# Wider column tiles and a folding matmul for the modulation rows of a two-layer diffusion trunk

## The reference, cut to what matters

```
sh1, sc1, g1, sh2, sc2, g2         = adaln(c,         ada_w[i], ada_b[i])   # silu(c) @ ada_w + ada_b, split in six
csh1, csc1, cg1, csh2, csc2, cg2   = adaln(c_ctx_row, ada_w[i], ada_b[i])
hl = modulate(rms_norm(xl, norm1_g[i]), sh1, sc1)
xl = xl + g1 * mixer(...);  xl = xl + g2 * conv_ffn(modulate(rms_norm(xl, norm2_g[i]), sh2, sc2), ...)
```

## Time and profile before

| | |
|---|---|
| median of 3 runs | 1913.11 us |
| profiled execution, time | 1913.11 us |
| profiled execution, span from first to last instruction | 1911.3 us |
| mean granted TensorE clock | 0.984 of 2.4 GHz |
| TensorE busy | 95% of the span |
| VectorE, ScalarE, GpSimd busy | 60%, 35%, 4% |
| modulation products L485 | 1536 records (768 matmuls) |
| modulation turns L478 | 24 records |

### The profile page before, as it was taken

The page is one execution under the profiler, slowest core; times in us unless marked ns, Lnnn a source line. Parts: engine busy times, 40 slices in busy tenths (PEclk is TensorE's granted clock), DMA queues, the critical chain, the costliest instruction groups (busy, mean ns, idle before and its releaser), DMA issues.

```text
span 1911.3 us, 29443 instructions
## 1 busy us (share of the span) xinstructions
PE 1815.1 (95%) x12484; PEld 1563.5 (82%) x12484; DVE 1150.3 (60%) x1917; ACT 676.9 (35%) x1007; POOL 79.5 (4%) x146
## 2 busy tenths in 40 slices
PE   3999999999977999999999999999888999999997
PEld 3999999999966878888888888878655888888885
DVE  3465576657684486633655256567555498487485
ACT  3333334433422243312332123334677243233242
POOL 0000000000040000000000000000353000000000
PEclk8999999999998999999999999999999999999998
DMA  7221221122101123233333233212100223222322
GB/s 295 85 82 67 89 84 62 67 89 89 57 34 34 56 79 124 96 102 119 111 112 109 89 122 110 78 60 87 34 1 1 88 78 99 99 91 98 99 92 107
DMA packets 45346, 166.03 MB, mean 87 GB/s; under 512 B 4897, under 2 KB 5281, under 8 KB 45089
## 3 DMA queue, kind: packets, MB, share of 16 engines
q1 hardware_dynamic: 45216, 164.16, 24.9%
HBM read 162.05 MB, written 2.10 MB: 86 GB/s over the span
## 4 chain that ended last, share of the span: by engine, by line
PE 87%; DVE 7%; ACT 2%; issue 1%; DMA 1%; SPq 0%; POOL 0%; DVEq 0%; ACTq 0%
PE slot L428 31%; PE slot L417 9%; PE slot L419 8%; PE slot L418 8%; PE slot L845 4%; PE slot L847 4%; PE slot L846 4%; PE MA L585 3%; PE MB L485 2%; PE MA L847 2%; PE MA L846 2%; PE MA L845 2%; PE slot L798 1%; DMA AD<-in_ada 1%; DVE Y L1346 1%
## 5 line engine op out<-in xcount | busy, mean ns | idle before, releaser
L1260 DVE TENSOR_TENSOR WL<-WR,WH 128x1024 fp32r<-128x1024 f32 x204 | 249.4, 1224 | 223.6 <-ACT WH L900 222.4
L900 ACT ACTIVATE WH<-WR 128x1024 fp32r<-128x1024 f32 x204 | 215.4, 1056 | 381.3 <-DMA WR<-in_w 381.1
L417 PE MATMUL slot<-HH,WH 128*128 128x384 f32 (+2 forms) x848 | 302.6, 357 | 18.9 <-DVE HL L1353 11.3
L418 PE MATMUL slot<-HL,WH 128*128 128x384 f32 (+2 forms) x848 | 293.3, 346 | 0.0
L419 PE MATMUL slot<-HH,WL 128*128 128x384 f32 (+2 forms) x848 | 293.2, 346 | 0.0
L428 PE MATMUL slot<-HH,WH 128*128 128x256 f32 (+1 forms) x816 | 212.6, 342 | 2.5 <-DVE ACC L1580 1.6
L428 PE MATMUL slot<-HH,WL 128*128 128x256 f32 (+1 forms) x816 | 210.8, 340 | 0.0
L428 PE MATMUL slot<-HL,WH 128*128 128x256 f32 (+1 forms) x816 | 208.9, 338 | 0.0
L417 PEld LDWEIGHTS slot<-HH,WH 128*128 128x128 f32 x848 | 161.0, 190 | 38.8 <-issue 17.8
L428 PEld LDWEIGHTS slot<-HH,WH 128*128 128x128 f32 x816 | 151.8, 189 | 26.1 <-issue 7.1
L428 PEld LDWEIGHTS slot<-HL,WH 128*128 128x128 f32 x816 | 154.0, 189 | 18.1
(11 more groups left out here) (222 smaller groups left out, 2985.2 us busy)
## 6 DMA issues: line engine op xcount, KB each, us to landing
WR<-in_w SPq DMA_DIRECT2D x204, 512.0 KB, 3.4
ada_raw<-in_ada SPq DMA_DIRECT2D x84, 512.0 KB, 4.6
AD<-in_ada SPq DMA_DIRECT2D x3, 2048.0 KB, 23.5
X<-in_x SPq DMA_DIRECT2D x1, 3072.0 KB, 12.3
out<-Y SPq DMA_DIRECT2D x8, 256.0 KB, 2.2
Y<-in_masks SPq DMA_DIRECT2D x1, 512.0 KB, 19.7
rope<-in_rope SPq DMA_DIRECT2D x1, 512.0 KB, 4.1
small<-in_small SPq DMA_DIRECT2D x1, 327.5 KB, 3.0
```

What stands on the lines that cost most here:

```text
L417: mm(SLOT[s][:, po], WH[w % NB][:, k, :], hi[:, k, to], start=(k == 0), stop=False)
L418: mm(SLOT[s][:, po], WH[w % NB][:, k, :], lo[:, k, to], start=False, stop=False)
L900: go(WH[t % NB][:, :, :], WR[t % NB][:, :, :], ACT.Copy).then_inc(w_hi_done, 1)
L1260: tt(WL[t % NB][:, :, :], WR[t % NB][:, :, :], WH[t % NB][:, :, :].bitcast(F32), ALU.subtract).then_inc(w_split, 1)
```

## The change

Three things are laid out differently; the values computed are the same.

1. In `ada_products` the column tile is no longer chosen by the piece of the output but by the block of input channels: each matmul multiplies one block of 128 channels with all 512 output columns and accumulates in partitions 32f to 32f+31 (f is the number of the block modulo 4). A group is 8 matmuls of 512 columns instead of 32 of 128 columns. The four partial sums lie one below the other in PSUM.
2. The copy by ScalarE takes 128x512 instead of 128x128.
3. The turn becomes four float32 matmuls. Piece m of the row block (128x128) is the stationary operand, and the moving operand is `fold`, a 128x2 matrix with ones where the partition modulo 32 equals the column. This adds the four partial sums and transposes at once; eight useful values per partition land in `MB[:, 512:520]`. VectorE makes `fold` from the identity with three small additions before the first squares, and TensorE waits for it once.

```
-                turn(MB[:, 512:512 + P], ada_row(rows.now(1))[:, 0:P], ident[:, :]).then_inc(ada_turned, 1)
+                for m in range(4):
+                    last = mm(MB[:, 512 + 2 * m:514 + 2 * m], ada_row(rows.now(1))[:, m * P:(m + 1) * P], fold[:, :], start=True, stop=True)
+                last.then_inc(ada_turned, 1)
 ...
                 for f in range(4):
                     c = 2 * k + f
-                    for m in range(4):
-                        last = mm(MB[32 * m:32 * m + 32, 0:P], silu_w[:, c, :], src(f)[:, m * P:(m + 1) * P], start=(c == 0), stop=(c == KC - 1))
+                    last = mm(MB[32 * f:32 * f + 32, 0:512], silu_w[:, c, :], src(f), start=(k == 0), stop=(k == 2))
 ...
-                    pe.wait_ge(ident_in_done, 16)
+                    pe.wait_ge(fold_ready, 1)
 ...
-                go(ada_row(rows.now(1))[:, 0:P], MB[:, 0:P], ACT.Copy).then_inc(ada_copied, 1)
+                go(ada_row(rows.now(1))[:, 0:512], MB[:, 0:512], ACT.Copy).then_inc(ada_copied, 1)
 ...
-                go(ada_row(g)[:, 0:P], MB[:, 0:P], ACT.Copy).then_inc(ada_copied, 1)
+                go(ada_row(g)[:, :], MB[:, 0:512], ACT.Copy).then_inc(ada_copied, 1)
 ...
-                tt(ada[:, j:j + 4, :], MB[:, 512:512 + P].rearrange("p (m x) -> p m x", x=32)[:, :, 0:2],
+                tt(ada[:, j:j + 4, :], MB[:, 512:520].rearrange("p (m v) -> p m v", v=2),
 ...
+            link(tt(fold[:, :], ident[:, 0:2], ident[:, 32:34], ALU.add))
+            link(tt(fold[:, :], fold[:, :], ident[:, 64:66], ALU.add))
+            tt(fold[:, :], fold[:, :], ident[:, 96:98], ALU.add).then_inc(fold_ready, 1)
```

More of the change, by code:

```diff
@@ L132, in trunk @@
         silu_w = sb("silu_w", [P, KC, 32])
+        fold = sb("fold", [P, 2])
         ada = sb("ada", [P, 96, 2])
@@ L156, in trunk @@
             AD0 = sb("AD0", [P, 4 * ADA_FIRST - 4, 2, 512], F32, s)
-            row0 = sb("row0", [P, P], F32, s)
+            row0 = sb("row0", [P, 512], F32, s)
         with ExitStack() as s:
@@ L176, in trunk @@
             ACC = [sb(f"ACC{i}", [P, TOK], F32, s) for i in range(2)]
-            row2 = sb("row2", [P, P], F32, s)
+            row2 = sb("row2", [P, 512], F32, s)
         with ExitStack() as s:
@@ L221, in trunk @@
         sig_ready, silu_ready, lb_shifted = sem("sig_ready"), sem("silu_ready"), sem("lb_shifted")
+        fold_ready = sem("fold_ready")
         ada_copied, ada_turned, ada_ready = sem("ada_copied"), sem("ada_turned"), sem("ada_ready")
```

## The result

The changed kernel takes 1933.9 us (median of 5 runs, 1929.02 to 1937.39), the kernel before, run beside it, 1912.98 us (median of 5). The ratio is 1.0102, 95% interval 1.0084 to 1.0121: 1% slower, some 19.5 us. The forecast was 1928 us.

The account below looks back on a forecast made before the run. TensorE was taken to bound the kernel. Products -0.6, turns +14.2 and prologue +1.0 us summed to +14.6 us on 1913.1 us, giving 1927.7 us, stated as 1928 us; range 1921 to 1938 us.

Parts of the forecast that it names:

- What bounds it: Background: TensorE, busy 95% of the span; each nanosecond added there lengthens the kernel, for 18 of the 20 turns.
- The two covered turns: Head steps: two turns stand ahead of TensorE waits of 6.5 and 2.1 us, where 0.8 us each vanish.
- Products, -0.6 us: Background half groups: two waves instead of eight, 1.00 us, gaining 0.015 us per half, 0.6 us for 40 halves.
- Turn, +0.79 us each, +14.2 us: Background turns: eight records at 0.11 us replace one, +0.79 us each, +14.2 us for 18 turns.
- Copy, nothing: ScalarE's background copy: 0.60 us, +0.32 us, but several us ahead of its turn, so no cost.
- Prologue, +1.0 us: Prologue: first big product 2.0 us later, 1.0 us given back by less half-clock time, net +1.0 us.
- the one on the clock: Prologue: the granted clock, at half from 30.63 us, rises at 37.44 us as before.
- The worse case of the prediction, +5.6 us: Prologue: without the clock's rise at 37.44 us, first products may run at half for longer; +5.6 us at most.
- the high end: Range's upper end, 1938 us: bad prologue with one stretch of lost clock and a few us for the copy.
- a turn that costs 0.5 us: In-between case of the rival that small matmuls are nearly free: 1922 us; chance 0.09 for all within 0.5%.
- the cheap turn: Faster rival, chance 0.04: turns at their cheap end, +2.3 us in all; faster from a wave under 0.30 us.

Follow-up runs that it names:

- prologue alone: The 4 prologue groups as in the changed kernel, the 20 background groups as in the kernel before: 1919.86 us, ratio 1.0028.
- background alone: The 20 background groups as in the changed kernel, the 4 prologue groups as in the kernel before: 1929.68 us, ratio 1.0095.
- filled changed kernel: The changed kernel plus idle-time matmuls in the prologue, results not read (2 after the second turn, 13 after the spread): 1930.19 us, ratio 1.0093 to the kernel before.

## Why the prediction was right, point by point

The time, 1933.9 us, lies in the range (1921 to 1938), 6 us above the forecast; the sign, the cause and the bulk of the size are as forecast.

- **What bounds it**: right. With TensorE 95% busy and no wait around 18 of the 20 turns, its added time came through: +14.0 us from the first background half group to behind the last turn, where +13.7 us of pieces are measured. The two covered turns vanished in the waits of L605, 0.7 us each instead of 0.8.
- **Products, -0.6 us**: right. 0.996 against 1.011 us for a half group, 40 x 0.015 = 0.6 us. Two waves of four at two cycles a column; the run with two tiles shows what overlap they rest on.
- **Turn, +0.79 us each, +14.2 us**: right. +0.78 us in the feed-forward, +0.83 us in the head steps: 12 x 0.78 + 6 x 0.83 = 14.3 us. The row from which it was priced, L512 at 0.11 us, is the same kind of record; the runs with 32 stationary and with 64 moving columns show that it is the load that is paid.
- **Copy, nothing**: right. 0.60 us as worked out, and the run with the wide copy and the old turn is not slower.
- **Prologue, +1.0 us**: the term that was mis-sized. The profile has +5.15 us at the first background half group, the profile of the prologue alone +5.8 us. The step that failed is the one on the clock: that it would be at half from 30.63 to 37.44 us as before. It was at half from 30.09 to 40.33 us, and again from 43.74 us. So the fourth group started 2.5 us late (1.75 us were forecast) and ended 2.7 us late (0.9 us), since it found no full clock; the last spread began 3.7 us late (2.0 us) and took 0.5 us more; and the first big products, instead of giving back 1.0 us, ran at half until 57.4 us and lost another 1.0 us. The worse case of the prediction, +5.6 us, is near what came, but by another way: its own terms (1.75, 0.2, 0.3, 1.6 and 1.0 us) add up to 4.9 us, not to the 4.5 us that it states, and its last turn, put at half clock, ran at full.

The clock's rise and fall were treated as fixed in time. They were not: the nine profiles of kernels without fillers have the first fall that they show at 29.66 to 44.90 us, and two of them with the same prologue instructions, before and background alone, have it at half for 6.8 and for 3.4 us. What sets it is open, and with it how much of the 5 us is the clock and how much the longer turns and copies.

That the time lies in the range is in part luck of its width: the high end was set by the worse prologue. With 5.15 us in place of 1.0 the sum is 13.7 + 5.15 = 18.9 us, against the 20.3 us by which the spans differ and 19.5 us by the ratio.

Two side sums of the rivals are off and change nothing: a turn that costs 0.5 us (0.39 us more) would give 1920.5 us, not 1922 us, and with the cheap turn a wave must be under 0.27 us, not 0.30 us, for the kernel to be faster.

## What to carry to other kernels

Price each of the two records of a float32 matmul by the larger of its two sides, as measured here at full clock: 0.11 us for the load of 128 stationary columns, however few columns it streams (2 or 64), and two cycles a column for those that it streams (0.109 us for 128, 0.43 us for 512). Fewer, wider matmuls saved 0.015 us of 1.01 us where the four column tiles were already full, and a transpose of one record (0.11 us) was cheap compared with four matmuls that fold and transpose at once (0.89 us). If such a fold is needed, cut its stationary operand into 32 columns in four column tiles: 0.36 us instead of 0.81, though the whole kernel is then still 0.4% slower than with the plain transpose.

Don't read differences of 3 or 4 us between two profiles of such a kernel as the effect of an edit before the same stretches have been laid side by side.

## What the runs showed of the hardware that was not expected

- The records of float32 matmuls in four column tiles start in waves of four, 6 to 7 ns apart within a wave (4, then 8 of them in the earlier trace rows), and in two tiles in waves of two, although two records belong to each matmul and to the same tile. It looks as if tiles took records out of the program's order; that isn't shown, since the trace doesn't name a record's tile. The time from wave to wave is about that of one record: 0.109 us for 128 columns, 0.43 us for 512 with four tiles and 0.42 to 0.45 us with two.
- The granted clock stayed at half for 13.65 us while TensorE was busy for over 90% of the time (the filled changed kernel), and rose after shorter stretches elsewhere. With the old prologue the first big product started at 47.57 and 46.11 us, with the new one at 51.75 and 52.25 us, and at 51.29 us with 64 moving columns in the turn: with only a few profiles of each, an effect in the prologue is known to 1 or 2 us.
- The big products of the feed-forward need 3.5 us more from the first turn to the last in the kernel with the prologue alone changed (468.15 against 464.62 us, background of the same form), yet executions of the same background agree to 0.01 us (464.62 twice; 473.31 us in the changed kernel, its filled form and the background alone). So it goes with the kernel and not with the execution; by what, no run here shows.
